# Borders of a two-block transformer's second block in token halves, adds and three pooled tiles on GpSimd, down products waiting row by row

## The chip, the cores and the metric

One core of a Trainium2 chip runs the whole kernel in one launch. The metric is the device time of one execution in microseconds (us). TensorE multiplies matrices into PSUM; VectorE, ScalarE and GpSimd do elementwise work; SyncE issues the loads of weights and the stores of the result. Each engine works through its own queue in order, and they hand work to each other by semaphores.

## The reference

Two transformer blocks in a row, all in float32, width 1024, feed-forward width 2816. The first runs on 512 tokens. The second puts 16 meta tokens in front of them (528 tokens) and has two layers, each the same frame around another mixer:

```python
for i in range(DEPTH_2):                       # i = 0: attention, i = 1: pooling
    a = rmsnorm(h, norm_mix_pre[i])
    m = mla_mixer(a, ...) if i % N_MIXERS == 0 else pool_mixer(a, pool_w_group[j], pool_scale[j])
    h = h + rmsnorm(m, norm_mix_post[i])
    f = conv_ffn(rmsnorm(h, norm_ffn_pre[i]), ffn_w_up[i], ffn_conv_w[i], ffn_conv_b[i], ffn_w_down[i])
    h = h + rmsnorm(f, norm_ffn_post[i])
```

`pool_mixer` takes, for each quarter of the channels, the mean over the last 2, 4, 8 or 16 tokens, subtracts the token itself and multiplies by a 256x256 matrix. `conv_ffn` is an up product, a causal three-tap convolution over tokens, silu(gate) * value, and a down product. `rmsnorm` divides a token by the root of the mean of its squares: a sum over channels, which lie on partitions here.

## The kernel before

Activations lie with channels on partitions and tokens along the free axis, so x is eight tiles of 128 channels by 528 tokens (512 in the first block). An exact float32 product is made of three (`mm3`, L426): both operands are split into a rounded part and its remainder, and w_lo·x_hi, w_hi·x_lo and w_hi·x_hi are added in PSUM. 528 tokens are two spans of 264, so each product of the second block is drawn as two MATMUL rows.

The weights come as a stream of 128x1024 blocks in a ring of four slots (`RING`). For each block SyncE loads `w_raw` (`load_w`), ScalarE rounds it to `w_hi` (`upper`, L883, some 1.04 us) and GpSimd makes the remainder `w_lo` (`lower`, L809, "a lowering" in what follows, some 2.4 us); TensorE waits for `w_lo_ok` of the block and gives the slot back with `w_used`. `STAGES` lists them in order:

```python
    ("dqkv", 6, 1), ("uq", 4, 2), ("uk", 2, 1), ("uv", 2, 1), ("wo", 4, 2),
    ("up_b", 4, 11), ("down_b", 12, 2), ("pool", 2, 1), ("up_c", 4, 11), ("down_c", 12, 2),
```

The numbers are the blocks in one turn of a loop and its turns. A turn fills four PSUM tiles (four output tiles of 128 channels), so `up_b` makes its 44 output tiles in 11 turns and `down_b` its 8 in 2. A block of an up stage or of `wo` holds two rows (2 x 128 input channels) for four output tiles; of the 12 blocks of a down turn ten hold two rows and two hold one (`DOWN_ROWS`: 22 rows in all). Up and down stages of the first block are `up_a` and `down_a`. The four PSUM banks each carry one tile, and `free` counts when one has been read.

Between up and down stands the convolution: per output tile ScalarE takes PSUM with bias (L1099), VectorE adds the three taps (L1563, the longest of its steps) and gates (L1569), ScalarE rounds the result to `mid_hi`, VectorE makes `mid_lo` (L1573). Before the first down product TensorE waits for the whole of it:

```python
                pe.wait_ge(midl_ok, mid0 + KF + 1)
```

After `wo`, `down_b`, `pool` and `down_c` the second block has what is called a border here. ScalarE copies PSUM to `m_out` and squares it (`take_squared`); VectorE adds the squares of the first four tiles (`add_four`, L1595 to L1602); TensorE multiplies ones by that sum and by the last four squares (`norm_four`, L705), which puts the sum over channels in every partition; ScalarE takes Ln and Exp of it and VectorE refines the root into `RS` (`norm`). Then VectorE does all of `post`: for each of eight tiles a product with gain and root (L1611) and the add to x (L1614). A second norm of the new x follows (squares on ScalarE, ones-matmuls at L485), and `split` makes h: product and remainder on VectorE (remainder L1284), rounding on ScalarE. Behind `down_b` the split is that of the pooling (`pooled`, L1699 for its shifted adds), then two blocks of products (`pool`), and a border again before `up_c`. After `down_c` `post` is the last work, and SyncE stores each x tile as it is added.

On GpSimd nothing but lowerings stands from `wo` to the end.

## Time and profile before

| | us |
|---|---|
| median of 3 runs | 2363.22 (2359.76 to 2364.97) |
| span of the profiled execution | 2363.4 |
| TensorE busy in it | 2080.7 |
| VectorE, ScalarE, GpSimd busy | 978.9, 976.8, 836.2 |
| HBM read over it | 183.13 MB, 78 GB/s |

The profile lists one execution. Its span is within 0.2 us of the median of the timed runs. Busy times are those of an engine's own instructions, over the whole span; they say nothing yet of which one is waited for at a given place.

### The profile page before, as it was taken

The page shows a single profiled execution, that of the slowest core. Times are in us where ns is not written, and L with a number is a line of the kernel's source. Part 1 is how long each engine was busy: PE and PEld are TensorE (multiplying, and loading weights), DVE is VectorE, ACT ScalarE, POOL GpSimd, SP SyncE. Part 2 cuts the span into 40 slices and gives each one's busy share as a digit, 9 for nine tenths or more (in the row PEclk, how much of TensorE's full clock was granted, in tenths as well). Part 3 has the DMA queues.
Part 4 walks back from the last instruction along what each step waited for, and adds up shares of the span by engine and source line. Part 5 has one row for each costly group of instructions (what it writes and reads, how often), then busy time and mean ns, then how long its engine had stood idle before and what let it go on. Part 6 is the DMA issues. An engine that isn't in the chain of part 4 may idle for free.

```text
span 2363.4 us, 35671 instructions
## 1 busy us (share of the span) xinstructions
PE 2080.7 (88%) x12776; PEld 1823.4 (77%) x12780; DVE 978.9 (41%) x1644; ACT 976.8 (41%) x1500; POOL 836.2 (35%) x415
## 2 busy tenths in 40 slices
PE   3699999998899989966878897999899659999897
PEld 2587677876577777756767797999899549999896
DVE  5863682114433421155667716242400672424102
ACT  2212673322655542143356634454512344545322
POOL 1244442433244334402643221434334104343341
PEclk7899899999999999988989998999999779999998
DMA  8362001222022222201200011222222102222222
GB/s 295 119 246 101 7 17 38 90 89 71 33 101 89 89 85 101 100 34 45 83 16 0 0 63 36 98 80 98 80 84 101 39 18 89 80 97 80 80 98 80
DMA packets 54263, 185.99 MB, mean 79 GB/s; under 512 B 6848, under 2 KB 8128, under 8 KB 54208
## 3 DMA queue, kind: packets, MB, share of 16 engines
q1 hardware_dynamic: 52768, 183.66, 22.1%
q10 hardware_dynamic: 1440, 1.59, 0.2%
q8 instruction: 35, 0.57, 0.1%
q14 instruction: 20, 0.16, 0.0%
HBM read 183.13 MB, written 2.10 MB: 78 GB/s over the span
## 4 chain that ended last, share of the span: by engine, by line
PE 76%; DVE 13%; issue 5%; ACT 3%; POOL 1%; DMA 1%; DVEq 0%; ACTq 0%; SPq 0%; POOLq 0%
PE PS L426 62%; PE PS L577 3%; PE PS L520 3%; PE PS L646 2%; PE PS L485 1%; PE PS L550 1%; DVE X L1614 1%; DVE small L1413 1%; DVE work L1611 1%; DVE work L1563 1%; PE PS L473 1%; DVE ada_acc L1312 1%; DVE X L1535 1%; PE PS L623 1%; DMA ada_w<-ada 1%
## 5 line engine op out<-in xcount | busy, mean ns | idle before, releaser
L809 POOL TENSOR_TENSOR w_lo<-w_raw,w_hi 128x1024 fp32r<-128x1024 f32 x289 | 697.7, 2418 | 1311.2 <-ACT w_hi L883 1310.0
L883 ACT ACTIVATE w_hi<-w_raw 128x1024 fp32r<-128x1024 f32 x293 | 309.9, 1058 | 884.2 <-PE PS L426 807.7
L426 PE MATMUL PS<-H_hi,w_lo 128*128 128x264 f32 (+1 forms) x2152 | 568.7, 323 | 60.3 <-DVE H_lo L1284 44.9
L426 PE MATMUL PS<-H_hi,w_hi 128*128 128x264 f32 (+1 forms) x2152 | 562.2, 320 | 0.0
L426 PE MATMUL PS<-H_lo,w_hi 128*128 128x264 f32 (+1 forms) x2152 | 561.5, 319 | 0.0
L426 PEld LDWEIGHTS PS<-H_hi,w_lo 128*128 128x128 f32 x2152 | 360.8, 192 | 104.8 <-issue 54.8
L1563 DVE SCALAR_TENSOR_TENSOR work<-PS,vec,work 128x526 f32<-128x526 f32 (+3 forms) x264 | 188.6, 756 | 482.3 <-ACT work L1099 472.5
L426 PEld LDWEIGHTS PS<-H_hi,w_hi 128*128 128x128 f32 x2152 | 360.2, 192 | 27.3
L426 PEld LDWEIGHTS PS<-H_lo,w_hi 128*128 128x128 f32 x2152 | 360.0, 191 | 25.9
L426 PE MATMUL PS<-mid_hi,w_lo 128*128 128x264 f32 (+1 forms) x880 | 215.9, 311 | 21.9 <-DVE mid_lo L1573 20.1
L426 PE MATMUL PS<-mid_hi,w_hi 128*128 128x264 f32 (+1 forms) x880 | 214.5, 309 | 0.0
L426 PE MATMUL PS<-mid_lo,w_hi 128*128 128x264 f32 (+1 forms) x880 | 214.5, 309 | 0.0
L426 PEld LDWEIGHTS PS<-mid_hi,w_lo 128*128 128x128 f32 x880 | 144.7, 191 | 31.3 <-issue 21.0
L426 PEld LDWEIGHTS PS<-mid_lo,w_hi 128*128 128x128 f32 x880 | 144.9, 191 | 7.9
L426 PEld LDWEIGHTS PS<-mid_hi,w_hi 128*128 128x128 f32 x880 | 144.3, 191 | 7.8
L1099 ACT ACTIVATE work<-PS,vec 128x528 f32<-128x528 f32 (+1 forms) x132 | 104.1, 788 | 80.9 <-PE PS L426 80.9
L485 PE MATMUL PS<-work,ones 128*128 128x264 f32 (+1 forms) x212 | 75.7, 512 | 53.2 <-ACT work L929 53.2
L1012 ACT ACTIVATE work<-PS,small 128x128 f32<-128x128 f32 (+5 forms) x144 | 78.6, 546 | 100.9 <-DVE small L1413 100.8
L485 PEld LDWEIGHTS PS<-work,ones 128*128 128x128 f32 x212 | 44.1, 220 | 84.7 <-issue 63.9
L1413 DVE TENSOR_REDUCE small<-PS 128x1 f32<-128x128 f32 (+5 forms) x144 | 73.2, 508 | 49.2 <-PE PS L535 49.1
L520 PE MATMUL PS<-k_hi,q_lo 64*128 64x256 f32 (+2 forms) x192 | 75.4, 393 | 17.2 <-POOL k_lo L835 16.5
L1264 DVE TENSOR_SCALAR work<-PS 128x528 f32<-128x528 f32 (+1 forms) x14 | 9.8, 698 | 194.4 <-ACT work L937 194.4
(212 smaller groups left out, 2924.2 us busy)
## 6 DMA issues: line engine op xcount, KB each, us to landing
w_raw<-stream SPq DMA_DIRECT2D x293, 512.0 KB, 3.2
ada_w<-ada SPq DMA_DIRECT2D x48, 512.0 KB, 5.9
X<-xT SPq DMA_DIRECT2D x1, 2048.0 KB, 8.9
yT<-X SPq DMA_DIRECT2D x8, 256.0 KB, 2.0
rel_raw<-rel ACTq DMA_DIRECT2D x8, 128.0 KB, 2.0
vec<-vecs SPq DMA_DIRECT2D x1, 390.0 KB, 2.8
cos_t<-rope ACTq DMA_DIRECT2D x1, 264.0 KB, 2.5
sin_t<-rope ACTq DMA_DIRECT2D x1, 264.0 KB, 3.0
```

The lines of the kernel that those rows point to most:

```text
L426: last = pe.matmul(out[:, c0 + a:c0 + b], w, x[:, a:b], start=start and i == 0, stop=stop and i == 2)
L473: last = pe.matmul(PS[:, 1, c0 + a:c0 + b], ones[:, :], x[:, a:b], start=k == first, stop=k == n - 1)
L485: last = pe.matmul(PS[:, 0, c0 + a:c0 + b], ones[:, :], square[:, a:b], start=k == 0, stop=k == n - 1)
L520: pe.matmul(out[0:qn, c0 + a:c0 + b], l[rows, o + q0:o + q0 + qn], r[rows, o + a:o + b], start=j == 0, stop=False, skip_group_check=True)
L577: last = pe.matmul(PS[:, 3, 256 + a:256 + b], l[0:kn, vo:vo + P], r[0:kn, so + a:so + b], start=par == 0 and j == 0 and n_ == 0, stop=par ...
L646: last = pe.matmul(PS[:, t, 0:512], l[:, hs], r[:, wr], start=kt == 0 and j == 0, stop=kt == 7 and j == 2)
L809: gp.tensor_tensor(w_lo[:, o], w_raw[:, o], w_hi[:, o].bitcast(F32), ALU.subtract)\
L883: return act_.activation(out, in_, ACT.Copy, scale=scale)
L1012: act_.activation(ht(work, t % 2, S2)[0:qn, 0:ke], PS[0:qn, t % 2, c0:c0 + ke], ACT.Exp, bias=small[0:qn, t % 2:t % 2 + 1], accum_out=smal ...
L1099: act_.activation(ht(work, m, T), psumT(m, T), ACT.Identity, bias=v1("conv", g * 16 + (c + 3)), scale=v1("conv", g * 16 + (c + 2)))\
L1413: v.tensor_reduce(small[0:qn, t % 2:t % 2 + 1], PS[0:qn, t % 2, c0:c0 + ke], AX.X, ALU.max, negate=True).then_inc(nmax_ok, 1)
L1563: ins = v.scalar_tensor_tensor(y[:, s:], u[:, :T - s], w, y[:, s:], ALU.mult, ALU.add)
```

## The change

It touches five things.

- `DOWN_ROWS` puts the two one-row blocks of a down turn first, and the down products wait for `midl_ok` one row at a time, in all three feed-forward parts.
- In the second block the last four weight blocks of `wo`, `down_b` and `down_c` are multiplied twice, each time with half of the tokens (0 to 263, then 264 to 527: half a and half b), and so are the first four blocks behind `wo` and `pool`, and both blocks of `pool` (`tail`, `head`, `pool_half`). The sum of squares of half a stands behind the first block of the second pass.
- Norms, products with gain and root, adds to x, squares and h are made per half, so the operations have 264 columns instead of 528 and there are twice as many.
- The adds to x are GpSimd's (`add_x`, L1077), VectorE keeps the products (`weigh`, L1978).
- GpSimd makes pooled tiles 0, 1 and 2 and their remainders (`pooled_gp`, L1087 to L1112, and `lower_gp`, L1117), VectorE tiles 3 to 7. The result leaves in 16 stores.

The core of the diff; the DVE and ACT parts follow the same order as the GpSimd and PE parts:

```diff
-DOWN_ROWS = (2,) * (KF - 12) + (1,) * (24 - KF)
+DOWN_ROWS = (1,) * (24 - KF) + (2,) * (KF - 12)
...
+HALVES = ((0, HALF2), (HALF2, S2))
...
+POOL_GP = (0, 1, 2)
+POOL_DVE = (3, 4, 5, 6, 7)
...
+            def ffn1(up, down, T, h0):
...
-                pe.wait_ge(midl_ok, mid0 + KF + 1)
...
-                    batch(down, 0, g, g * 12 + BLK0[down], range(12), 4, DOWN_ROWS, 4,
-                          lambda k: (ht(mid_hi, k, T), ht(mid_lo, k, T)), T)
+                    batch(down, 0, g, g * 12 + BLK0[down], range(12), 4, DOWN_ROWS, 4, mid(T), T,
+                          (midl_ok, 1))
...
+                for s in range(2):
+                    done = r0
+                    for b in range(nb - 4, nb):
+                        first, final = b == 0, b == nb - 1
+                        last = half_block(n0 + b, s, rows[b], done, x, first, final,
+                                          begin_tile=(lambda m: begin(name, 0, m, 1)) if first else None,
+                                          told=(4 - s) * final, teller=tail_ok[s])
+                        if s:
+                            last.then_inc(w_used, 1)
+                        done += rows[b]
+                        if s == 1 and b == nb - 4:
+                            sum_squares(name, 0)
...
+            def head(name, before, s, h_base):
+                for b in range(4):
+                    def begin_tile(m):
+                        if s == 0:
+                            bank_free(before, m, 0)
+                        else:
+                            begin(name, 0, m, 0)
+                    def h_wait(k):
+                        pe.wait_ge(hh_ok[s], h_base + k + 1)
+                    last = half_block(BLK0[name] + b, s, 2, 2 * b, hx(S2), b == 0, b == 3,
+                                      begin_tile=begin_tile if b == 0 else None, told=3 * (s == 1 and b == 3),
+                                      teller=full, h_wait=h_wait)
+                    if s == 0 and b == 2:
+                        sum_x_squares(before, 1)
+                    if s:
...
+            def ffn2(up, down, mid0):
+                with pe.Fori(1, 11) as g:
+                    batch(up, 0, g, g * 4 + BLK0[up], range(4), 4, 2, 4, hx(S2), S2)
+                batch(down, 0, 0, BLK0[down], range(12), 4, DOWN_ROWS, 4, mid(S2), S2, (midl_ok, mid0 + 1))
+                tail(down, mid(S2), DOWN_ROWS)
+            batch("wo", 0, 0, BLK0["wo"], range(4), 4, 2, 4, ox2, S2)
+            tail("wo", ox2, (2,) * 4)
+            sum_x_squares("wo", 0)
+            sum_squares("wo", 1)
+            head("up_b", "wo", 0, 0)
+            head("up_b", "wo", 1, 0)
+            ffn2("up_b", "down_b", KF)
+            sum_x_squares("down_b", 0)
+            sum_squares("down_b", 1)
+            pool_half(0)
+            sum_squares("pool", 0)
+            sum_x_squares("down_b", 1)
+            sum_x_squares("pool", 0)
+            pool_half(1)
+            sum_squares("pool", 1)
+            head("up_c", "pool", 0, KD + len(POOL_DVE))
+            head("up_c", "pool", 1, KD + len(POOL_DVE))
+            ffn2("up_c", "down_c", 2 * KF)
...
+            def add_x(name, s):
+                j = TAIL_N[name]
+                for k in range(KD):
+                    gp.wait_ge(wm_ok[s], j * KD + k + 1)
+                    gp.tensor_tensor(hf(X, k, s), hf(X, k, s), hf(work, k % 2, s), ALU.add).then_inc(xh_ok[s], 1)
...
+            def pooled_gp(s):
+                a, b = HALVES[s]
+                gp.wait_ge(rs2_ok[s], 2 * TAIL_N["down_b"] + 2)
+                gp.wait_ge(pad_ok, 2)
+                for k in POOL_GP:
+                    gchain.done(gp.tensor_tensor(padded(k, a, b), X[:, k * S2 + a:k * S2 + b], RS[:, a:b], ALU.mult))
+                for k in POOL_GP:
+                    gchain.wait(2)
+                    gchain.done(gp.tensor_scalar(padded(k, a, b), padded(k, a, b), v1("mix_pre", KD + k),
+                                                 0.5 if k < 2 else 1.0, ALU.mult, ALU.mult))
+                for k in (0, 1):
+                    gchain.wait(2 - k)
+                    a1 = max(a, 1)
+                    gp.tensor_tensor(pool_o[:, k * S2 + a1:k * S2 + b], padded(k, a1 - 1, b - 1), padded(k, a1, b),
+                                     ALU.subtract).then_inc(tp_ok[s], 1)
+                two, four = KD + POOL_SUM0[2], KD + POOL_SUM0[2] + 1
+                gchain.wait()
+                gchain.done(gp.tensor_tensor(padded(two, a, b), padded(2, a, b), padded(2, a - 1, b - 1), ALU.add))
+                gchain.wait()
+                gchain.done(gp.tensor_tensor(padded(four, a, b), padded(two, a, b), padded(two, a - 2, b - 2), ALU.add))
+                gchain.wait()
+                o = pool_o[:, 2 * S2:3 * S2]
+                if s == 0:
+                    i = VEC["cnt"] + 16
+                    gchain.done(gp.tensor_tensor(o[:, 0:16], padded(four, 0, 16), vec[:, i:i + 16], ALU.mult))
+                    a0 = 16
+                else:
+                    a0 = a
+                gchain.done(gp.tensor_scalar(o[:, a0:b], padded(four, a0, b), 0.25, None, ALU.mult))
+                gchain.wait()
+                gp.tensor_tensor(o[:, a:b], o[:, a:b], padded(2, a, b), ALU.subtract).then_inc(tp_ok[s], 1)
...
+            lower_blocks(BLK0["wo"] + RING, BLK0["up_b"])
+            add_x("wo", 0)
+            for b in range(3):
+                lower_one("up_b", b)
+            add_x("wo", 1)
+            lower_blocks(BLK0["up_b"] + 3, BLK0["pool"])
+            add_x("down_b", 0)
+            lower_one("pool", 0)
+            lower_one("pool", 1)
+            pooled_gp(0)
+            lower_one("up_c", 0)
+            lower_gp(0)
+            add_x("down_b", 1)
+            add_x("pool", 0)
+            lower_one("up_c", 1)
+            pooled_gp(1)
+            lower_gp(1)
+            lower_one("up_c", 2)
+            add_x("pool", 1)
+            lower_blocks(BLK0["up_c"] + 3, NBLK)
+            add_x("down_c", 0)
+            add_x("down_c", 1)
...
+            take_first("wo")
+            last_uppers("wo")
+            take_half("wo", 0)
+            root(0, 1)
+            next_upper("wo", 0)
+            square_x("wo", 0, range(0, 4))
+            next_upper("wo", 1)
+            square_x("wo", 0, range(4, 8))
+            next_upper("wo", 2)
+            take_half("wo", 1)
+            next_upper("wo", 3)
+            before_up("wo", 0)
...
-            def post(gain, i0, x0):
...
-                    chain.done(v.scalar_tensor_tensor(w, ht(m_out, k, S2), v1(gain, i0 + k), RS[:, :],
-                                                      ALU.mult, ALU.mult))
-                    chain.wait()
-                    v.tensor_tensor(x2(k), x2(k), w, ALU.add).then_inc(x_ok, 1)
...
+            def weigh(name, s, gain, i0, k):
+                j = TAIL_N[name]
+                if TAILS[name][1] == 8 or k >= 4:
+                    wait_half_out(v, name, s, k if TAILS[name][1] == 8 else k - 4)
+                if k >= 2:
+                    v.wait_ge(xh_ok[s], j * KD + k - 1)
+                v.scalar_tensor_tensor(hf(work, k % 2, s), hf(m_out, k, s), v1(gain, i0 + k), hf(RS, 0, s),
+                                       ALU.mult, ALU.mult).then_inc(wm_ok[s], 1)
...
+            def before_up(name, gain, i0, base, h0, p0):
+                c = 2 * TAIL_N[name]
+                root(0, c + 2)
+                for k in range(KD + 1):
+                    if k < KD:
+                        make_h(0, base, p0, k)
+                    if k == 2:
+                        root(1, c + 1)
+                    if k:
+                        lower_h(0, base, h0, k - 1)
+                    if k >= 3:
+                        weigh(name, 1, gain, i0, k - 3)
+                for k in range(KD - 2, KD):
+                    weigh(name, 1, gain, i0, k)
+                root(1, c + 2)
+                for k in range(KD + 1):
+                    if k < KD:
+                        make_h(1, base, p0, k)
+                    if k:
+                        lower_h(1, base, h0, k - 1)
...
+            def pooled_dve(s):
+                pooled(v, chain, (3,), s, th_ok[s])
+                pooled(v, chain, (4, 5), s, th_ok[s])
+                lower_pooled(s, (3,))
+                pooled(v, chain, (6, 7), s, th_ok[s])
+                lower_pooled(s, (4, 5, 6, 7))
```

What stands in the queues now, at three places. TensorE before the first product of `down_a`, with L680 the wait for the whole of mid (`free0` says that PSUM bank 0 is read), before:

```order
L680 UNCONDITIONAL_BRANCH [waits midl_ok]
L680 ISA
L432 REGISTER_ALU [waits w_lo_ok]
L426 MATMUL PS<-mid_hi,w_lo 128x512 [waits free0]
L426 MATMUL PS<-mid_lo,w_hi 128x512
L426 MATMUL PS<-mid_hi,w_hi 128x512
L426 MATMUL PS<-mid_hi,w_lo 128x512
L426 MATMUL PS<-mid_lo,w_hi 128x512
```

and in the changed kernel:

```order
L772 UNCONDITIONAL_BRANCH
L772 ISA
L522 REGISTER_ALU [waits w_lo_ok]
L516 MATMUL PS<-mid_hi,w_lo 128x512 [waits midl_ok,free0]
L516 MATMUL PS<-mid_lo,w_hi 128x512
L516 MATMUL PS<-mid_hi,w_hi 128x512
L522 REGISTER_ALU
L516 MATMUL PS<-mid_hi,w_lo 128x512 [waits free1]
L516 MATMUL PS<-mid_lo,w_hi 128x512
L516 MATMUL PS<-mid_hi,w_hi 128x512
L516 MATMUL PS<-mid_hi,w_lo 128x512 [waits free2]
```

The wait for `midl_ok` has moved from ahead of the loop to the first product of a row, and with one row in the first block four tiles are begun after three products each.

TensorE at the end of `wo` (OK_hi and OQ_lo are the attention's output, L705 are ones-matmuls), before:

```order
L426 MATMUL PS<-OQ_lo,w_hi 128x264 x2
L426 MATMUL PS<-OK_hi,w_hi 128x264 x2
L770 REGISTER_ALU
L770 COMPARE_AND_BRANCH
L705 MATMUL PS<-RS,ones 128x264 [waits sum4_ok,n_rs,free0]
L705 MATMUL PS<-RS,ones 128x264
L705 MATMUL PS<-work,ones 128x264 [waits n_sq]
L705 MATMUL PS<-work,ones 128x264
```

and in the changed kernel, once in the second pass of the last four blocks and once where the stage ends (`sqx` are squares of x, `mo_a` says that half a of a bank is read, `hh_ok_a` that half a of an h tile is there):

```order
L516 MATMUL PS<-OQ_lo,w_hi 128x264
L516 MATMUL PS<-OK_hi,w_hi 128x264
L806 MATMUL PS<-RS,ones 128x264 [waits sum4_ok,mo_a]
L809 MATMUL PS<-work,ones 128x264 [waits sqm_ok_a] x4
L516 MATMUL PS<-OK_hi,w_lo 128x264 [waits w_lo_ok]
L516 MATMUL PS<-OQ_lo,w_hi 128x264
L516 MATMUL PS<-OK_hi,w_hi 128x264
...
L516 MATMUL PS<-OK_hi,w_hi 128x264
L817 MATMUL PS<-sqx,ones 128x264 [waits sqx_ok_a,mo_a]
L817 MATMUL PS<-sqx,ones 128x264 [waits sqx_ok_a] x7
L806 MATMUL PS<-RS,ones 128x264 [waits sum4_ok,free0]
L809 MATMUL PS<-work,ones 128x264 [waits sqm_ok_b] x4
L516 MATMUL PS<-H_hi,w_lo 128x264 [waits hh_ok_a,mo_a,w_lo_ok]
L516 MATMUL PS<-H_lo,w_hi 128x264
```

The sum of squares of half a has moved in between products of half b; behind the last product stand eight ones-matmuls for the second norm of half a and five for the first norm of half b, and then `up_b` begins with products of half a.

GpSimd behind the attention, before:

```order
L835 TENSOR_TENSOR v_lo<-v_raw,v_hi 128x5x64
L827 REGISTER_ALU
L827 COMPARE_AND_BRANCH
L809 TENSOR_TENSOR w_lo<-w_raw,w_hi 128x1024 [waits w_hi_ok]
L818 UNCONDITIONAL_BRANCH
L818 ISA
L809 TENSOR_TENSOR w_lo<-w_raw,w_hi 128x1024 [waits w_hi_ok]
```

and, in the changed kernel, from `down_b` to the pooling of half b:

```order
L1077 TENSOR_TENSOR X<-X,work 128x264 [waits wm_ok_a] x8
L1009 TENSOR_TENSOR w_lo<-w_raw,w_hi 128x1024 [waits w_hi_ok] x2
L1087 TENSOR_TENSOR pool_s<-X,RS 128x264 [waits pad_ok,rs2_ok_a]
L1087 TENSOR_TENSOR pool_s<-X,RS 128x264 x2
L1090 ISA
L1090 TENSOR_SCALAR pool_s<-pool_s,vec 128x264 [waits gp_step] x3
L1095 TENSOR_TENSOR pool_o<-pool_s 128x263 [waits gp_step] x2
L1099 TENSOR_TENSOR pool_s<-pool_s 128x264 [waits gp_step]
L1101 TENSOR_TENSOR pool_s<-pool_s 128x264 [waits gp_step]
L1106 TENSOR_TENSOR pool_o<-pool_s,vec 128x16 [waits gp_step]
L1110 TENSOR_SCALAR pool_o<-pool_s 128x248
L1112 TENSOR_TENSOR pool_o<-pool_o,pool_s 128x264 [waits gp_step]
L1009 TENSOR_TENSOR w_lo<-w_raw,w_hi 128x1024 [waits w_hi_ok]
L1117 TENSOR_TENSOR H_lo<-pool_o,H_hi 128x264 [waits hi_ok_a] x3
L1077 TENSOR_TENSOR X<-X,work 128x264 [waits wm_ok_b] x8
L1077 TENSOR_TENSOR X<-X,work 128x264 [waits wm_ok_a] x8
L1009 TENSOR_TENSOR w_lo<-w_raw,w_hi 128x1024 [waits w_hi_ok]
L1087 TENSOR_TENSOR pool_s<-X,RS 128x264 [waits pad_ok,rs2_ok_b]
```

Where the loop of lowerings ran on to the end, 24 adds, the 13 steps of half a's pooling and 3 remainders stand among four lowerings, and the pooling's steps wait for one another (`gp_step`).

## Rows read from the trace of the kernel before

**Rows 1.** The page: span, and part 1, busy time of each engine.

```profile
span 2363.4 us, 35671 instructions
PE 2080.7 (88%) x12776; PEld 1823.4 (77%) x12780; DVE 978.9 (41%) x1644; ACT 976.8 (41%) x1500; POOL 836.2 (35%) x415
```

**Rows 2.** Windows over up_b, down_b, gap: busy PE, PEld, DVE, ACT, POOL; PEclk, DMA, GB/s.

```profile
1444.00:1705.00 261.00, 261.00 (x2111) 259.32 (x2110) 93.93 (x136) 134.50 (x153) 102.71 (x43) 0.99 0.25 85
1712.00:1843.00 131.00, 131.00 (x1056) 131.00 (x1057) 4.11 (x3) 31.43 (x35) 56.50 (x24) 0.98 0.26 90
1843.00:1941.00 98.00, 49.89 (x202) 39.27 (x200) 73.54 (x118) 37.72 (x59) 8.18 (x4) 0.75 0.07 25
```

**Rows 3.** Timeline where up_b ends: start, us, engine, line, work [idle before <-releaser].

```profile
1704.40 4.37 DVE L1563 SCALAR_TENSOR_TENSOR work<-PS,vec,work 128x526 f32<-128x526 f32 x6 [0.15 <-DVE work L1563]
1711.81 2.36 POOL L809 TENSOR_TENSOR w_lo<-w_raw,w_hi 128x1024 fp32r<-128x1024 f32 x1 [8.79 <-ACT w_hi L883]
1712.00 0.81 PE L426 MATMUL PS<-mid_hi,w_lo 128*128 128x264 f32 x2 [6.73 <-DVE mid_lo L1573]
```

**Rows 4.** Timeline of the border behind wo, VectorE and GpSimd.

```profile
1394.84 2.59 POOL L809 TENSOR_TENSOR w_lo<-w_raw,w_hi 128x1024 fp32r<-128x1024 f32 x1 [4.56 <-ACT w_hi L883]
1395.21 2.79 DVE L1602 TENSOR_TENSOR RS<-RS,work 128x528 f32<-128x528 f32 x1
...
1424.83 0.71 DVE L1614 TENSOR_TENSOR X<-X,work 128x528 f32<-128x528 f32 x1
1425.45 0.76 DVE L1611 SCALAR_TENSOR_TENSOR work<-m_out,vec,RS 128x528 f32<-128x528 f32 x1
```

**Rows 5.** Groups by form: busy us, mean ns of one | idle before.

```profile
L809 POOL TENSOR_TENSOR w_lo<-w_raw,w_hi 128x1024 fp32r<-128x1024 f32 x289 | 697.7, 2418 | 1311.2 <-ACT w_hi L883 1310.0 <-POOL Q L856 1.2
L883 ACT ACTIVATE w_hi<-w_raw 128x1024 fp32r<-128x1024 f32 x293 | 309.9, 1058 | 884.2 <-PE PS L426 807.7 <-PE PS L646 37.8 <-DMA w_raw<-stream 25.8
...
L835 POOL TENSOR_TENSOR q_lo<-Q,q_hi 128x528 fp32r<-128x528 f32 x16 | 21.1, 1318 | 75.8 <-ACT q_hi L883 75.5 <-ACT k_hi L883 0.3
L835 POOL TENSOR_TENSOR rel_lo<-rel_raw,rel_hi 128x256 fp32r<-128x256 f32 x8 | 5.8, 730 | 5.4 <-ACT rel_hi L883 5.4
...
L1439 DVE TENSOR_TENSOR PT_lo<-PS,PT_hi 128x256 fp32r<-128x256 f32 x32 | 13.2, 412 | 0.0
L883 ACT ACTIVATE PT_hi<-PS 128x288 fp32r<-128x288 f32 x32 | 12.4, 388 | 0.0
```

**Rows 6.** The chain that ended last: the ones-matmuls behind down_b.

```profile
1843.20 4.46 PE PS L705 x20
```

**Rows 7.** Timeline of down_a: TensorE in its middle, VectorE at its end.

```profile
938.04 0.50 PE L426 MATMUL PS<-mid_hi,w_lo 128*128 128x512 f32 x1 [0.70 <-DVE work L1531]
...
940.82 0.50 PE L426 MATMUL PS<-mid_hi,w_lo 128*128 128x512 f32 x1 [1.12 <-DVE work L1531]
...
998.11 2.58 DVE L1535 SCALAR_TENSOR_TENSOR X<-X,work 128x512 f32<-128x512 f32 x1
...
1001.38 2.06 DVE L1535 SCALAR_TENSOR_TENSOR X<-X,work 128x512 f32<-128x512 f32 x1
```

**Rows 8.** Timeline, other stretches: where stages end and begin, and the pooling.

```profile
1415.74 1.05 PE L705 MATMUL PS<-RS,ones 128*128 128x264 f32 x4
...
1443.38 0.56 PE L426 MATMUL PS<-H_hi,w_lo 128*128 128x264 f32 x1 [6.01 <-DVE H_lo L1284]
...
1843.04 0.61 PE L705 MATMUL PS<-RS,ones 128*128 128x264 f32 x2
...
1893.21 1.45 DVE L1699 TENSOR_TENSOR pool_s<-pool_s 128x528 f32<-128x528 f32 x2
...
1941.31 0.56 PE L426 MATMUL PS<-H_hi,w_lo 128*128 128x264 f32 x1 [6.01 <-DVE H_lo L1284]
...
2341.20 0.61 PE L705 MATMUL PS<-RS,ones 128*128 128x264 f32 x2
```

**Rows 9.** Timeline: GpSimd in the first attention's set-up.

```profile
301.39 1.27 POOL L835 TENSOR_TENSOR k_lo<-QK,k_hi 64x512 fp32r<-64x512 f32 x1 [0.24 <-POOL q_lo L835]
```

459 lines of the change are left out of this document (328 added, 131 removed).

## The prediction

> **What bounds the kernel now.** I read the page first [rows 1]: TensorE is busy 88% of 2363.4 us in the profiled execution, so time can only come from where TensorE waits. The windows by stage [rows 2] say where, in the second block: the up and down products run without a hole (261.00 of 261.00 and 131.00 of 131.00 us, granted clock 0.98 to 0.99 of 2.4 GHz). Between `down_b` and `up_c` lie 98 us with 49.89 busy; the rows in order of time add some 28 us between `wo` and `up_b` and 22 behind `down_c` [rows 8], and 7 between each up and its down [rows 3]. The reader is to see that VectorE fills the 98 us (73.54 busy): its chain of norm, add, pooling and norm is what TensorE waits for. Last I read, in order of time too, a norm in which VectorE and GpSimd meet [rows 4]. The profiled span, 2363.4, stands at the median of the runs, 2363.2, so the sum is made from 2363.2.
>
> **Prices for 264 columns.** VectorE with two inputs took 0.412 us for 256 columns [rows 5]: 0.42, and 0.47 where a gain is read too, as 0.76 stands against 0.71 at 528 [rows 4]; an independent one starts 0.09 before the last has ended [rows 4], so 0.35 to 0.40 in a stream. ScalarE 0.388 for 288 [rows 5]: 0.39, 0.33 in a stream. GpSimd 0.730 for 256, 1.318 for 528 [rows 5]: 0.75. TensorE 0.124 per product (131.0/1056 [rows 2]), and 0.446 for one exact ones-matmul (4.46 us for ten of them, each drawn as two rows) [rows 6].
>
> **GpSimd and VectorE exclude each other.** A two-input add on VectorE beside a lowering took 2.79 us instead of 0.71, and ended 0.57 behind GpSimd's end; the lowering itself, asked for while VectorE was in such an add, took 2.59 [rows 4] where their mean is 2.42 [rows 5]. So all that the change puts on GpSimd adds to VectorE's two-input time: a product and an add cost 0.35 + 0.75, 1.1 us a tile and half, 8.9 for eight, where the kernel before takes 0.76 and 0.71 less the overlap, some 1.4 for a whole tile [rows 4], 0.7 a half. The Trainium skill, SBUF — State Buffer, "Who interferes with whom", says the same as a rule: the pair of ports is an exclusive lock, and the second to issue fully blocks. By that rule the trace agrees.
>
> **1. Down waits row by row, three junctions.** TensorE stood 6.73 us until `mid_lo` of the last group [rows 3]. Now it waits for a bank only. VectorE's taps run from 1704.40, 0.68 apart: bank 0 is free at 1705.2, bank 1 at 1705.9, bank 2 at about 1708.0, bank 3 at 1708.8. A tile of a one-row block is six products, 0.74 us, so tiles 0 and 1 fill to 1706.8 and tile 2 waits 1.2. Some 1.4 us stay: 5.3 saved, three times 15.9. The last rows land at 1712.0, and are wanted 60 us later. The ring of four holds 1+1+2+2 rows, 17.8 us, against ScalarE's queue, which is clear at 1711.8, when GpSimd gets its block [rows 3]. Bounds: 12 (4.0 each) and 18.
>
> **2. The end of `down_a`.** Its last two blocks had one row, 2.8 us, and lowerings came back to back into VectorE's residual: 2.58 and 2.06 for 512 columns, 0.69 by the 0.71 of 528 [rows 4, 7], and TensorE stood 0.70 and 1.12 us in the middle [rows 7]. With two rows last, a block takes 5.7 us and a lowering meets one or two residuals, not the queue of them: 1.8 in the middle, and 2.7 of the 3.3 at the end. 4.5; bounds 0 and 5.
>
> **3. `wo` to `up_b`.** Call 0 the first ones-matmul of before, 1415.74 [rows 8]. The last four blocks are now two passes of 96 x 0.124 = 11.9 us with a sum of five ones-matmuls, 2.2, inside the second. So the last product ends at +2.2 and half a is complete at 2.2 - 11.9 - 2.2 = -11.9. Its sum stands behind one block of the second pass (24 products, 3.0): -8.9 to -6.7. Root: Ln and Exp 0.42 each, three VectorE operations 0.46 each, hops: -4.1. Eight products and adds at 1.1: +4.8. What is queued behind these adds on GpSimd are three lowerings of `up_b`, and SyncE's loads behind those. ScalarE has, behind the squares of half a, two weight roundings (1.06 by their mean [rows 5], 0.96 in a stream) and eight reads of half b (0.33 each), 4.6 us, before it may start the second root, which takes 2.7 more with its wait for the sum: +12.9. Product, rounding and remainder of the first tile, 0.47 + 0.42 + 0.42 and hops, 2.0: the first product of `up_b` at +14.9. Before it came at +27.6 [rows 8]. That is 12.7 us earlier. But the 2112 products of up, 261 us before, now hold 3.6 us of b's sum of x² (8 x 0.446); half a's 72 first products wait 2.9 on tiles of h that cost VectorE 0.35 for the product, 0.35 for the remainder, 0.35 for half b's product and 0.75 of GpSimd's add; then 1.5 until half b's h, and 1.3 for a lowering that stood behind GpSimd's adds: 9.3. Net 3.4 saved. Bounds: 0 (nothing of the lead survives) and 7 (the holes of 5.7 go, and some).
>
> **4. `down_b` to `up_c`.** 0 is now 1843.04 [rows 8], and the start is the same: adds of half a from -4.1 to +4.9, second root at +12.4 (before, both norms were done at about +25). Then, in order of VectorE's queue:
> - Pooling of half a. VectorE has 26 full-width sums and products, 10 of 16 columns and 5 remainders; GpSimd 12 short ones of 264, one of 16, one lowering (2.4) and 3 remainders. GpSimd's run in turn with VectorE's: 15 x (0.75 + 0.22 of waiting) + 2.4 = 17; the rest of VectorE's behind it, 15 x 0.38 + 10 x 0.15 = 7.2; with hops 24.5: +37.
> - Root of half b 1.7, its eight products and adds 8.9, and 1.6 until the last squares: +49.
> - Root of the pool's half a, 2, and its eight adds, 8.9: +60.
> - Root of x in half b. A lowering of `up_c` takes the lock in the middle of it, 2.4: +63.
> - Pooling of half b, the same without the 16-column steps, 21: +84.
> - The pool's products of half b, 8 squares and 8 reads of ScalarE (0.33 to 0.4 each), a lowering, eight ones-matmuls and a root: +94. The first tile of h: first `up_c` product at +95.5.
>
> Before it came at 1941.31, +98.3 [rows 8]. So 2.8 us earlier, and again 9.3 lost inside the two passes of up, less an estimated 0.3 for a granted clock of 0.75 over the gap before [rows 2], which would be up sooner: 6.2 us slower. This is where the work on GpSimd is paid for: VectorE's 73.54 us become about 64, but some 60 of GpSimd can't lie beside them. Bounds: 10 faster (GpSimd hidden for half its time) and 20 slower (0.25 more for each of some 50 operations, and a hop each).
>
> **5. The end.** 22.2 us from the last sum of squares to the end [rows 1, 8]. Now half b: 2.2 later by the inserted sum, four weight roundings of ScalarE (0.96 each) ahead of the root, but eight adds at 1.1 instead of sixteen operations at 0.71, and a root at half width: 0.4 saved; bounds -3 and 3. The 16 output transfers of half the size replace 8; the first eight go out under half b, and the last is issued by its add as before.
>
> **Sum.** 15.9 + 4.5 + 3.4 - 6.2 + 0.4 = 18.0 us: 2363.2 - 18.0 = 2345. Unseen costs: GpSimd's one-input TENSOR_SCALAR, eight of them, taken at a two-input's 0.75 (nearest rows, and both bounds are its 256 columns 0.73 and a full 528 1.32: -0.2 to +4.6 us in all); reads at a shifted column, taken at nothing, as two shifted adds of VectorE took 1.45, 0.73 each [rows 8]. The Trainium skill, GPSIMD Engine Reference, "Engine selection", puts one-input operations at roughly line rate; by that the eight would be near 0.4 us as an estimate and the sum 2.6 better. No run here shows it.
>
> **Rivals.**
> - *The lock doesn't bite on short operations.* Then eight adds take 8 x 0.75 = 6, hidden under VectorE, and pooling overlaps: 1.1 to 0.75 over 64 adds is some 15 on the path, the two poolings 5 each: 25 us more, 2320. For it: no row has both engines in short ones. Against: the rows of 528 [rows 4] leave no overlap. Chance 0.10.
> - *The junctions give nothing.* A one-row block first leaves less cover, and the down product waits for a lowering that comes at 1711.81 + 2.36 [rows 3] and then each 2.4: against 17.8 us of blocks from 1705.3 there are 9 to spare, so I give it little. 2361. Chance 0.07.
> - *Slower: short GpSimd operations are dearer in a chain.* About 75 of 95 stand on the path. The hop after GpSimd was 0.24 where it waited for itself [rows 9]. At 0.25 us more each, 0.99 instead of 0.75, 18.8 us go and it decides; at 0.35 more the time is 2371. For it: per column the short form already costs more than the long (730/256 against 2418/1024 [rows 5]). Chance 0.08.
> - *Something in between*, half a junction lost or half a lock, 2352 to 2360: 0.07, of which 0.02 within 0.2%.
>
> **How the numbers follow.** The forecast, all five terms near their values, 2336 to 2354, has 0.68. The range 2328 to 2359 adds the milder parts of the neighbours and leaves out half of the first and most of the second and third rival, 0.2. What a measurement here can tell from no change is 0.2%, 4.7 us. Faster: 0.68 + 0.10 + 0.05 of the cases between + 0.02 of the second rival, where a part of the junctions stays = 0.85. Same: the other 0.05 of that rival and 0.02 between = 0.07. Slower 0.08.
>
> **What would show it.** At the junctions TensorE idles under 2 us for a bank. In the windows, `down_b` to `up_c` stays within a few us of 98 while VectorE's two-input operations read 0.9 to 1.1 us instead of 0.42, and GpSimd's adds 0.75 to 0.9. The first up product comes 12 us sooner after `wo`, and up takes 9 longer. VectorE rows of 0.42 beside GpSimd rows would prove the first rival; adds at 1 us with VectorE idle the slow one. I would be wrong above all by GpSimd's length, 7.5 us for each 0.1, and by the order in which the two take the lock.

## The result, and the profile after

The changed kernel took 2323.95 us (median of 4 runs, 2320.99 to 2328.26) beside 2362.18 for the kernel before: a ratio of 0.9842 with a 95% interval of 0.9827 to 0.9856, 38 us faster. The forecast was 18 us faster, 2345, in a range of 2328 to 2359: the direction was right, the size half of what was measured, and the time lies below the range. The profiled execution of the changed kernel took 2328.26 and has a span of 2326.4, so its trace shows 37.0 of the 38 us [rows 1].

The page of the changed kernel, span and part 1, against [rows 1]:

```profile
span 2326.4 us, 35857 instructions
PE 2070.3 (89%) x12792; PEld 1814.9 (78%) x12792; DVE 992.0 (43%) x1711; ACT 989.1 (43%) x1602; POOL 915.1 (39%) x510
```

GpSimd is busy 79 us longer and VectorE 13 us longer, and yet the kernel is faster. The windows of the changed kernel over the rest of `up_b`, `down_b` without its last pass, and from `down_b` to `up_c`, with the columns of [rows 2]:

```profile
1436.00:1688.00 252.00, 250.41 (x2034) 248.38 (x2032) 93.38 (x141) 133.57 (x155) 102.70 (x43) 1.00 0.29 90
1688.00:1809.00 121.00, 119.81 (x981) 119.53 (x981) 10.22 (x12) 35.54 (x44) 50.76 (x21) 1.00 0.30 95
1821.00:1905.00 84.00, 42.35 (x186) 35.15 (x184) 60.16 (x114) 37.91 (x94) 51.64 (x54) 0.78 0.09 32
```

The third row answers to the 98 us of [rows 2]: VectorE's 73.54 busy us have become 60.16, GpSimd's 8.18 have become 51.64, and the stretch is 13 us shorter. The second row shows a granted clock of 1.00 where `down_b` had 0.98.

TensorE and VectorE of the changed kernel at the end of `up_b`, in order of time, against [rows 3]:

```profile
1688.10 0.48 PE L516 MATMUL PS<-mid_hi,w_lo 128*128 128x264 f32 x2
...
1690.99 0.51 PE L516 MATMUL PS<-mid_hi,w_lo 128*128 128x264 f32 x2 [1.19 <-DVE work L1918]
...
1693.15 1.46 DVE L1928 TENSOR_TENSOR mid_lo<-work,mid_hi 128x528 f32 x2 [0.32 <-ACT mid_hi L1155]
```

The wait of 6.73 us is gone, 1.19 for a PSUM bank is left, and the last rows of mid come while down runs. And VectorE and GpSimd in the row of products and adds behind `wo`:

```profile
1401.24 1.37 DVE L1978 SCALAR_TENSOR_TENSOR work<-m_out,vec,RS 128x264 f32<-128x264 f32 x2 [0.64 <-POOL X L1077]
1403.33 1.30 DVE L1978 SCALAR_TENSOR_TENSOR work<-m_out,vec,RS 128x264 f32<-128x264 f32 x2 [0.72 <-POOL X L1077]
1405.36 1.31 DVE L1978 SCALAR_TENSOR_TENSOR work<-m_out,vec,RS 128x264 f32<-128x264 f32 x2 [0.72 <-POOL X L1077]
...
1402.29 1.65 POOL L1077 TENSOR_TENSOR X<-X,work 128x264 f32<-128x264 f32 x2 [0.37 <-DVE work L1978]
1404.31 1.65 POOL L1077 TENSOR_TENSOR X<-X,work 128x264 f32<-128x264 f32 x2 [0.37 <-DVE work L1978]
1406.34 1.63 POOL L1077 TENSOR_TENSOR X<-X,work 128x264 f32<-128x264 f32 x2 [0.37 <-DVE work L1978]
1407.93 6.97 POOL L1009 TENSOR_TENSOR w_lo<-w_raw,w_hi 128x1024 fp32r<-128x1024 f32 x3
```

GpSimd's pairs of adds repeat every 2.02 to 2.03 us, 1.01 a tile, and each engine waits for the other in turn. The three lowerings of `up_b` stand behind the eighth add.

From the rows at which stages end and begin, in the two profiled executions (us from the last product of one stage, taken where the ones-matmuls behind it start, to the first of the next, the 2.2 us of the sum of squares that was inserted into a stage counted with the border behind it; `down_b` to `up_c` before: 1843.04 to 1941.31 [rows 8], after: 1820.64 to 1905.38 and 2.2):

| part | forecast saved | before | after | saved |
|---|---|---|---|---|
| `up_a`'s end over `down_a` to `dqkv` | 5.3 + 4.5 | 176.8 | 166.4 | 10.4 |
| `up_b`'s end to `down_b`'s, and the same in c | 5.3 each | 137.8 each | 130.3 each | 7.5 each |
| `wo` | 0 | 49.7 | 48.3 | 1.4 |
| `wo` to `up_b` | 12.7 | 27.6 | 14.0 | 13.6 |
| `up_b` itself | -9.3 | 261.9 | 270.4 | -8.5 |
| `down_b` to `up_c` | 2.8 | 98.3 | 86.9 | 11.3 |
| `up_c` itself | -9.3 + 0.3 | 262.1 | 270.5 | -8.4 |
| `down_c` to the end | 0.4 | 22.2 | 20.2 | 2.0 |

The forecast column adds up to 18.0, the last to 36.8. An up stage "itself" is from its first product to its last.

### The profile page after: what moved, and what is told of

Same layout as the page of the kernel before. It is cut to its first block, busy times and chain, and to the rows that moved or that the text cites. A ratio compares the mean times of both kernels' runs of the same rounds, so it can differ in the third digit from the quotient of the medians.

```text
span 2326.4 us, 35857 instructions
## 1 busy us (share of the span) xinstructions
PE 2070.3 (89%) x12792; PEld 1814.9 (78%) x12792; DVE 992.0 (43%) x1711; ACT 989.1 (43%) x1602; POOL 915.1 (39%) x510
## 3 DMA queue, kind: packets, MB, share of 16 engines
q1 hardware_dynamic: 53920, 183.66, 24.5%
## 4 chain that ended last, share of the span: by engine, by line
PE 76%; DVE 12%; issue 5%; ACT 4%; POOL 2%; DMA 1%; DVEq 0%; ACTq 0%; POOLq 0%; SPq 0%
PE PS L516 62%; PE PS L667 3%; PE PS L610 3%; PE PS L736 2%; PE PS L640 1%; PE PS L575 1%; DVE work L1918 1%; DVE small L1768 1%; PE PS L563 1%; DVE ada_acc L1667 1%; DVE pool_s L292 1%; DMA ada_w<-ada 1%; POOL X L1077 1%; PE PS L960 1%; DVE work L1978 1%
## 5 line engine op out<-in xcount | busy, mean ns | idle before, releaser
L516 PE MATMUL PS<-H_hi,w_lo 128*128 128x264 f32 (+1 forms) x2152 | 583.3, 323 | 67.9 <-POOL H_lo L1117 27.5
L516 PE MATMUL PS<-H_hi,w_hi 128*128 128x264 f32 (+1 forms) x2152 | 576.0, 320 | 0.0
L516 PE MATMUL PS<-H_lo,w_hi 128*128 128x264 f32 (+1 forms) x2152 | 575.1, 319 | 0.0
L516 PEld LDWEIGHTS PS<-H_lo,w_hi 128*128 128x128 f32 x2152 | 366.5, 192 | 25.8
L516 PE MATMUL PS<-mid_hi,w_lo 128*128 128x264 f32 (+1 forms) x880 | 223.8, 308 | 3.6 <-DVE work L1918 3.6
L516 PE MATMUL PS<-mid_hi,w_hi 128*128 128x264 f32 (+1 forms) x880 | 222.8, 306 | 0.0
L516 PE MATMUL PS<-mid_lo,w_hi 128*128 128x264 f32 (+1 forms) x880 | 222.3, 306 | 0.0
L1768 DVE TENSOR_REDUCE small<-PS 128x1 f32<-128x128 f32 (+5 forms) x144 | 73.2, 509 | 49.4 <-PE PS L625 49.3
L1077 POOL TENSOR_TENSOR X<-X,work 128x264 f32<-128x264 f32 x64 | 53.8, 856 | 97.0 <-DVE work L1978 97.0
L640 PE MATMUL PS<-ident,work 128*128 128x128 f32 (+2 forms) x400 | 69.1, 280 | 23.6 <-DVE work L1779 22.4
L575 PE MATMUL PS<-work,ones 128*128 128x512 f32 (+1 forms) x116 | 47.0, 563 | 32.1 <-ACT work L1201 32.1
```

What stands on the lines that cost most here:

```text
L516: last = pe.matmul(out[:, c0 + a:c0 + b], w, x[:, a:b], start=start and i == 0, stop=stop and i == 2)
L575: last = pe.matmul(PS[:, 0, c0 + a:c0 + b], ones[:, :], square[:, a:b], start=k == 0, stop=k == n - 1)
L640: last = pe.transpose(PS[0:kn, 2, o:o + qn], pb[0:qn, k0:k0 + kn], ident[0:qn, 0:qn])
L1077: gp.tensor_tensor(hf(X, k, s), hf(X, k, s), hf(work, k % 2, s), ALU.add).then_inc(xh_ok[s], 1)
L1768: v.tensor_reduce(small[0:qn, t % 2:t % 2 + 1], PS[0:qn, t % 2, c0:c0 + ke], AX.X, ALU.max, negate=True).then_inc(nmax_ok, 1)
```

## The experiments

Ratios are to the kernel before, timed beside each.

**b_junction.** The kernel before with the first part of the change alone.

```diff
-DOWN_ROWS = (2,) * (KF - 12) + (1,) * (24 - KF)
+DOWN_ROWS = (1,) * (24 - KF) + (2,) * (KF - 12)
...
-                                pe.wait_ge(h_ok, h_ready + kt + 1)
+                                pe.wait_ge(r_sem or h_ok, h_ready + kt + 1)
...
-                pe.wait_ge(midl_ok, mid0 + KF + 1)
...
-                          lambda k: (ht(mid_hi, k, T), ht(mid_lo, k, T)), T)
+                          lambda k: (ht(mid_hi, k, T), ht(mid_lo, k, T)), T, mid0 + 1, midl_ok)
```

> The kernel before with the change's first part alone: down products wait for midl_ok row by row, one-row blocks first. Theory 1 (the prediction's terms 1 and 2): TensorE's wait of 6.7 us at each junction shrinks to 1.4, and the end of down_a gains 4.5: 15.9 + 4.5, about 20 us faster than before, 2342. Theory 2 (the wait also cost granted clock: the first 5 us of down products ran at 0.50): each junction gives 5.5 of wait and 2 of clock, with 3.8 at down_a some 26 us faster, 2336. The rest of the whole change (38 us) would then be worth 12 and not 18.

Measured: 2337.0 us, 0.9888 (0.9872 to 0.9903), 25 us faster. That is two thirds of the whole gain, and theory 2. The same stretch as above, `up_b`'s end to `down_b`'s, is 7.6 us shorter, of which the wait explains 5.5. The windows over `down_b` say where the rest is. Before, over the wait and the first 10 us behind it:

```profile
1705.00:1712.00 7.00, 0.27 (x4) 0.06 (x2) 6.21 (x10) 5.77 (x8) 0.19 (x1) 0.87 0.11 42
1712.00:1717.00 5.00, 5.00 (x22) 5.00 (x23) 0.00 (x0) 1.04 (x1) 2.17 (x1) 0.50 0.29 103
1717.00:1722.00 5.00, 5.00 (x42) 5.00 (x42) 0.00 (x0) 1.06 (x1) 0.42 (x1) 1.00 0.01 5
```

and with the junction alone, over the whole of `down_b`:

```profile
1693.50:1823.50 130.00, 128.79 (x1055) 128.58 (x1056) 10.02 (x12) 39.63 (x45) 57.96 (x24) 1.00 0.29 97
```

After 6.73 idle us TensorE's granted clock stood at 0.50, its level of 1.2 GHz, for the next 5 us: 22 product rows where the following 5 us hold 42. That is 20 rows of 0.12, over 2 us lost on top of the wait. The kernel before shows the same behind its waits for `mid` in the first block and in `up_c`:

```profile
872.40:877.40 5.00, 4.98 (x12) 3.93 (x13) 0.00 (x0) 1.09 (x1) 2.23 (x1) 0.51 0.27 105
2210.10:2215.10 5.00, 4.96 (x22) 4.97 (x23) 0.00 (x0) 1.07 (x1) 2.21 (x1) 0.50 0.31 103
```

After the 1.21 idle us of b_junction it stayed at 1.00. The mean of 0.98 over 131 us [rows 2] had hidden it.

**b_waits_only.** The same with `DOWN_ROWS` left as it was (two-row blocks first).

> As b_junction, but the one-row blocks stay last. The first block of a turn has then two rows, a tile takes 1.5 us instead of 0.74, and tile 2 comes after its bank is free: no wait at all is left at the junctions. Theory 1: 3 x 6.7, 20 us faster than before, nothing at the end of down_a. Theory 2: 3 x (6.7 + 2.1), 26 us, as much as b_junction, so that the order of the rows gives nothing in sum. If the order helps the end of down_a as the prediction had it (4.5) and costs 1.2 at each junction, the two kernels lie within 1 us of each other.

Measured: 2335.57 us, 0.9890 (0.9875 to 0.9905), 26 us faster, the same as b_junction. In the traces `down_b` is 1.5 us shorter (128.93 against 130.41 from first product to last, no wait for a bank), `down_c` as much, and the stretch behind `down_a` is 2.1 us longer and `down_a` 0.7. The order of the rows pays at one place, `down_a`, what it costs at the other two. The row by row wait is the whole of the gain.

**b_warm.** The kernel before keeps its wait, and TensorE works in it (on ones, the results overwritten).

```diff
+                pe.wait_ge(free[0], FREE0[down][0] + 1)
+                for i in range(24):
+                    pe.matmul(PS[:, 0, 0:128], ones[:, :], ones[:, 0:128], start=True, stop=True)
                 pe.wait_ge(midl_ok, mid0 + KF + 1)
```

> The kernel before with its wait for the whole of mid kept, but TensorE multiplies ones by ones (24 products of 128 columns into the free bank 0, results overwritten) while it waits. Theory 1: the wait is all that the junction costs, so the time stays at 2362. Theory 2: the granted clock stays at 1.0 behind the wait, the first 18 products of down take 0.12 us instead of 0.22, and each junction gives 2 us: 6 us faster, 2356.

Measured: 2357.07 us, 0.9980 (0.9971 to 0.9989), 5.0 us faster by work that is thrown away. Windows over the wait and the first 5 us of down products in b_warm:

```profile
1702.00:1708.70 6.70, 5.58 (x49) 5.39 (x48) 5.95 (x9) 5.74 (x8) 0.15 (x1) 1.00 0.06 24
1708.70:1713.70 5.00, 4.96 (x40) 4.97 (x41) 0.00 (x0) 1.07 (x1) 2.23 (x1) 1.00 0.29 93
```

The stretch from the last up product to the first down product is 6.73 us as before, and `down_b` takes 129.01 instead of 131.21, `down_c` 128.99 instead of 131.22, `down_a` 124.70 instead of 126.94: 2.2 each, 6.7 in sum; the interval of the timed runs, some 2.6 to 6.9 us, holds that sum. So the granted clock is a cost of its own.

**b_bench.** A bench behind the last add of the kernel before; the weights' buffers are its inputs. Per phase, VectorE and GpSimd run so many operations, with a barrier between phases. A phase lists for VectorE and then for GpSimd the kind, the columns and the number of operations; "tt" adds two tensors in SBUF, "ts" is a TENSOR_SCALAR with one tensor input, "ps" an add with one input in PSUM.

```diff
+        PHASES = (("tt", 264, 16, None, 0, 0), (None, 0, 0, "tt", 264, 8), ("tt", 264, 16, "tt", 264, 8),
+                  ("tt", 528, 8, "tt", 528, 4), ("tt", 264, 16, "tt", 1024, 3), (None, 0, 0, "ts", 264, 8),
+                  ("tt", 264, 16, "ts", 264, 8), ("ts", 264, 16, None, 0, 0), ("ts", 264, 16, "tt", 264, 8),
+                  ("ps", 264, 16, "tt", 264, 8), ("tt", 528, 8, None, 0, 0), (None, 0, 0, "tt", 528, 4))
```

> The kernel before with a bench behind its last add: VectorE and GpSimd in independent operations, alone and together, phase by phase with a barrier between. Widths 264, 528 and 1024. Theory A (the prediction's): each excludes the other for a whole operation: 16 VectorE adds (0.35 each) and 8 GpSimd adds (0.75 each) of 264 together take 16 x 0.35 + 8 x 0.75 = 11.6 us. Theory B (the rival): no exclusion on short operations, they take the longer of the two, 6 us. Theory C: exclusion only while data streams, some 0.27 of VectorE's 0.35 and some 0.5 of GpSimd's 0.75: 16 x 0.27 + 8 x 0.5, about 8.5 us. With GpSimd's input a lowering of 1024 columns, VectorE's short adds stand still for its whole 2.4 us in A and C alike. GpSimd's one-input operation: 0.75 by the prediction; VectorE from PSUM beside GpSimd: as alone.

It ran once, 2443.8 us with the bench; what counts are its rows, in order of time for VectorE (phases 1, 8 and 9 in one row, 10 and 11) and then for GpSimd (phases 2 to 7, 9, 10 and 12):

```profile
2358.55 5.59 DVE L303 TENSOR_TENSOR m_out<-w_hi 128x264 f32<-128x264 f32 x16 [0.23 <-DVEq L1746]
...
2412.94 12.62 DVE L299 TENSOR_SCALAR m_out<-w_hi,vec 128x264 f32<-128x264 f32 x32 [0.38 <-POOL XC L299]
2425.60 5.52 DVE L301 TENSOR_TENSOR m_out<-PS,w_hi 128x264 f32<-128x264 f32 x16
2431.38 5.04 DVE L303 TENSOR_TENSOR m_out<-w_hi 128x528 f32<-128x528 f32 x8 [0.26 <-POOL XC L303]
...
2364.36 5.61 POOL L303 TENSOR_TENSOR XC<-w_lo 128x264 f32<-128x264 f32 x8 [39.55 <-DVE m_out L303]
2370.43 6.95 POOL L303 TENSOR_TENSOR XC<-w_lo 128x264 f32<-128x264 f32 x8 [0.46 <-POOL XC L303]
2380.16 6.97 POOL L303 TENSOR_TENSOR XC<-w_lo 128x528 f32<-128x528 f32 x4 [2.77 <-DVE m_out L303]
2389.63 7.56 POOL L303 TENSOR_TENSOR XC<-w_lo 128x1024 f32<-128x1024 f32 x3 [2.50 <-DVE m_out L303]
2401.70 3.70 POOL L299 TENSOR_SCALAR XC<-w_lo,vec 128x264 f32<-128x264 f32 x8 [4.51 <-DVE m_out L303]
2405.57 7.26 POOL L299 TENSOR_SCALAR XC<-w_lo,vec 128x264 f32<-128x264 f32 x8 [0.17 <-POOL XC L299]
2417.54 6.01 POOL L303 TENSOR_TENSOR XC<-w_lo 128x264 f32<-128x264 f32 x8 [4.70 <-DVE m_out L299]
2425.65 5.63 POOL L303 TENSOR_TENSOR XC<-w_lo 128x264 f32<-128x264 f32 x8 [2.10 <-DVE m_out L299]
2436.65 5.05 POOL L303 TENSOR_TENSOR XC<-w_lo 128x528 f32<-128x528 f32 x4 [5.37 <-DVE m_out L303]
```

Alone, an add of 264 columns costs VectorE 0.35 and GpSimd 0.70. Together GpSimd's eight take 6.95 (0.87 each by their mean), and GpSimd starts its next phase, behind VectorE's sixteenth, 9.7 us after the first: between theory A's 11.6 and C's 8.5, and far from B's 6. In 6.95 us VectorE made nine, the other seven took the 2.77 us for which GpSimd then waited: they go in turn, and a pair costs 0.87 where the durations add up to 1.05. At 528 columns a pair costs 1.74 where 0.63 and 1.26 add up to 1.89. So the exclusion holds for short operations, less 0.15 to 0.18 per pair. The Trainium skill, SBUF — State Buffer, "Who interferes with whom", has the lock as exclusive; the bench agrees, but for that overlap. With one of VectorE's inputs in PSUM both run as alone (5.52 and 5.63). One-input operations of GpSimd cost 0.46 alone and 0.91 beside VectorE's adds. A one-input operation on VectorE isn't free of GpSimd either: VectorE's TENSOR_SCALAR costs 0.27 alone (sixteen from 2412.94 until GpSimd starts its phase 9), and GpSimd's eight adds beside them took 6.01, 0.75 for a pair. The Trainium skill, GPSIMD Engine Reference, "Engine selection", puts GpSimd's one-input operations at roughly line rate and its two-input ones about twice as slow as VectorE's. The bench agrees on the second, 0.70 against 0.35 alone; with one tensor input it was 0.46 against VectorE's 0.27.

**a_add_dve.** The changed kernel with the add to x back on VectorE, behind its product.

```diff
                 for k in range(KD):
-                    gp.wait_ge(wm_ok[s], j * KD + k + 1)
-                    gp.tensor_tensor(hf(X, k, s), hf(X, k, s), hf(work, k % 2, s), ALU.add).then_inc(xh_ok[s], 1)
...
                                        ALU.mult, ALU.mult).then_inc(wm_ok[s], 1)
+                v.wait_ge(wm_ok[s], j * KD + k + 1)
+                v.tensor_tensor(hf(X, k, s), hf(X, k, s), hf(work, k % 2, s), ALU.add).then_inc(xh_ok[s], 1)
```

> The changed kernel with the adds to x back on VectorE: product, wait for it, add, tile by tile and still in halves. Theory S (GpSimd's adds stop VectorE for most of their length, so moving them gives nothing): a tile and half costs 0.93 us (two dependent VectorE operations at 0.46) where product and GpSimd's add now repeat every 1.01; over five rows of eight on the path 3 us faster than the changed kernel, and up to 1 lost where h tiles stand between: 2321 to 2325. Theory M (taking the adds off VectorE is a real gain): each add returns 0.35 to 0.42 us to VectorE's chain, 40 of them on the path, 14 to 17 us slower, about 2339.

Measured: 2330.89 us, 0.9863 (0.9848 to 0.9878), slower than the changed kernel by some 5 to 7 us in median, with intervals that overlap. The stages are clearer (table below): 3.0 lost behind `wo`, 4.1 behind `down_b`, 1.1 won at the end. Neither theory holds: S had the sign wrong, and M's 14 to 17 us were 7 or less and came, as the rows show, from something else. The row of eight behind `wo` on VectorE, and GpSimd beside it:

```profile
1397.05 2.50 DVE L1976 SCALAR_TENSOR_TENSOR work<-m_out,vec,RS 128x264 f32<-128x264 f32 x1
...
1399.94 0.49 DVE L1976 SCALAR_TENSOR_TENSOR work<-m_out,vec,RS 128x264 f32<-128x264 f32 x1
1400.46 0.43 DVE L1979 TENSOR_TENSOR X<-X,work 128x264 f32<-128x264 f32 x1
1400.81 0.49 DVE L1976 SCALAR_TENSOR_TENSOR work<-m_out,vec,RS 128x264 f32<-128x264 f32 x1
...
1404.30 2.58 DVE L1976 SCALAR_TENSOR_TENSOR work<-m_out,vec,RS 128x264 f32<-128x264 f32 x1
...
1396.64 2.63 POOL L1009 TENSOR_TENSOR w_lo<-w_raw,w_hi 128x1024 fp32r<-128x1024 f32 x1 [13.87 <-ACT w_hi L1153]
1404.13 2.47 POOL L1009 TENSOR_TENSOR w_lo<-w_raw,w_hi 128x1024 fp32r<-128x1024 f32 x1 [4.86 <-ACT w_hi L1153]
```

Undisturbed, a tile takes 0.87 us on VectorE alone, less than the 1.01 with GpSimd. But GpSimd, free of adds, goes on with its lowerings as soon as their weights are rounded, and each holds up a product by 2 us.

**a_pool_dve.** The changed kernel with all pooled tiles on VectorE.

```diff
-POOL_GP = (0, 1, 2)
-POOL_DVE = (3, 4, 5, 6, 7)
+POOL_GP = ()
+POOL_DVE = (0, 1, 2, 3, 4, 5, 6, 7)
...
-            pooled_gp(0)
...
-            pooled_gp(1)
```

> The changed kernel with all eight pooled tiles and their remainders on VectorE, GpSimd only lowers. Theory S: the pooling of a half is then 44 VectorE operations at 0.35 and, in half a, 16 short ones at 0.1, 17.5 and 15.5 us, where it took 21 and 17.5 with both engines: some 5 us faster than the changed kernel, 2319; as little as 2 if lowerings now fall into it. Theory M: the 13 and 12 steps and 3 remainders that GpSimd made were hidden in part; VectorE's share grows by 16 operations of 0.35 a half, 2 x 5.6, so 8 to 11 us slower, 2333.

Measured: 2321.5 us, 0.9826 (0.9812 to 0.984), not told apart from the changed kernel by its time, but its `down_b` to `up_c` is 3.05 us shorter. From the root to the last remainder half a took 17.9 us (21.0 with both engines) and half b 15.7 (17.5). Half b, in whose pooling neither kernel has a lowering, shows the tiles alone: 1.8. In half a something else moved too. The changed kernel has a lowering of `up_c` in the middle of VectorE's pooling:

```profile
1840.59 2.53 POOL L1009 TENSOR_TENSOR w_lo<-w_raw,w_hi 128x1024 fp32r<-128x1024 f32 x1
1840.84 2.57 DVE L285 SCALAR_TENSOR_TENSOR pool_s<-X,vec,RS 128x264 f32<-128x264 f32 x1
```

Here it comes ahead of the pooling and holds up a step of the root instead (1.77 for 0.43):

```profile
1819.05 6.97 POOL L1009 TENSOR_TENSOR w_lo<-w_raw,w_hi 128x1024 fp32r<-128x1024 f32 x3
1824.54 1.77 DVE L1962 SCALAR_TENSOR_TENSOR work<-work 128x264 f32<-128x264 f32 x1
```

By the stages, the three tiles given to GpSimd cost more than they relieve; how much of half a's 3.1 us is the tiles and how much the lowering's place was not separated.

**a_none_gp.** Both edits together.

> Both: halves and row by row waits, but neither adds nor pooled tiles on GpSimd. Theory S: the two gains add, 4 to 9 us faster than the changed kernel, 2315 to 2320, and the halves alone are then worth the whole of the 12 us that the junctions leave and more. Theory M: 20 us or more slower than the changed kernel, 2345, which is slower than the kernel before with the junctions alone (2337).

Measured: 2326.51 us, 0.9851 (0.9837 to 0.9864). The two don't add: behind `wo` it loses what a_add_dve lost (table below). But it says what the token halves are worth by themselves, with the row by row waits and everything but lowerings off GpSimd: against b_junction (2337.0, 0.9872 to 0.9903) it is some 10 us faster, with intervals that lie apart.

**a_warm.** The changed kernel with products of ones in three waits: eight behind the last sum of squares after `wo`, ten ahead of each half of `pool`.

```diff
+            def keep_busy(n, s):
+                for _ in range(n):
+                    pe.matmul(psum_half(3, s), ones[:, :], vec[:, 0:HALF2], start=True, stop=True)
```

> The changed kernel with products of ones in three of TensorE's waits (8 behind wo's last sum of squares, 10 ahead of each half of pool, into a bank that is free, results overwritten). Where the clock is 0.50 at a start, the products of half a pool stage (96 rows) take 0.22 instead of 0.12. Theory clock: both pool halves end 3 to 4 us sooner, of which ScalarE's and VectorE's queues leave about half, and up_b begins 1 us sooner in its second block: 3 to 7 us faster, 2317 to 2321. Theory wait (the pool stage and the heads wait for VectorE's tiles, whatever the clock): no change within 2 us of 2324, or slower if the extra products hold up the real ones.

Measured: 2326.72 us, 0.9857 (0.9842 to 0.9872), no gain. The waits of its TensorE over the two pool halves:

```profile
PE PS L516 <- ACT m_out L1168: 8.3, 2, 4.2
PE PS L873 <- ACT H_hi L1168: 5.7, 1, 5.7
PE PS L817 <- ACT sqx L1283: 3.6, 4, 1.4
```

(us in total, times, longest.) The first block of a pool half ran at 1.00, then TensorE waited 4 us for ScalarE to read its banks and the second block ran at 0.62 in the mean. There the clock follows the waits, and the waits set the time; `down_b` to `up_c` was 1.0 us longer.

**a_add_gated.** As a_add_dve, and GpSimd waits where it added.

```diff
-                for k in range(KD):
-                    gp.wait_ge(wm_ok[s], j * KD + k + 1)
-                    gp.tensor_tensor(hf(X, k, s), hf(X, k, s), hf(work, k % 2, s), ALU.add).then_inc(xh_ok[s], 1)
+                gp.wait_ge(xh_ok[s], (j + 1) * KD)
```

> As a_add_dve (adds to x back on VectorE), but GpSimd, where it added before, now waits until VectorE has added all eight tiles of the half, and only then goes on with its lowerings. Theory Q (the adds on GpSimd helped by what they kept out: lowerings, each of which held a VectorE product for 2.5 us in a_add_dve): with the lowerings kept out and a tile at 0.87 us on VectorE against 1.01 before, up_b starts 10.7 us after wo's last product (11.8 in the changed kernel, 14.8 in a_add_dve) and up_c 81 to 82 after down_b's (84.7 and 88.9); 4 to 6 us faster than the changed kernel, 2319. Theory M (an engine of its own for the adds is the gain): as a_add_dve, 2331.

Measured: 2323.16 us, 0.9834 (0.982 to 0.9847). Against a_add_dve (0.9863, 0.9848 to 0.9878) an idle GpSimd makes the kernel faster, by intervals that are just apart. `up_b` starts 10.73 us after `wo`'s last product, as expected; `up_c` starts at 83.2 and not at 81 to 82.

**a_gated.** As a_add_gated, with all pooled tiles on VectorE.

> As a_add_gated, and all pooled tiles on VectorE: GpSimd does nothing but lowerings, at the places that the changed kernel gave them. Theory Q: the gain of a_add_gated and the 3 us of a_pool_dve together, up_c starts 78 to 79 us after down_b's last product, 7 to 9 us faster than the changed kernel, 2316. If the two gains don't add (a lowering or ScalarE's reads take the place), 81 and 2320.

Measured: 2319.71 us (2318.68 to 2322.23), 0.9820 (0.9807 to 0.9833), the lowest of all, though not told apart from a_pool_dve (0.9826). It is apart from a_none_gp (0.9851, 0.9837 to 0.9864), from which it differs by GpSimd's wait alone. Against the changed kernel the intervals overlap a little; by stages it is 1.1, 3.2 and 1.1 us shorter. The gains added in part only: 81.55.

From the traces, us (last product to first product, and to the end):

| kernel | `wo` to `up_b` | `down_b` to `up_c` | `down_c` to the end |
|---|---|---|---|
| changed | 11.82 | 84.74 | 17.9 |
| a_add_dve | 14.80 | 88.87 | 16.8 |
| a_pool_dve | 11.81 | 81.69 | 17.9 |
| a_none_gp | 14.79 | 83.25 | 16.8 |
| a_add_gated | 10.73 | 83.19 | 16.8 |
| a_gated | 10.74 | 81.55 | 16.8 |

A stage ends where the ones-matmuls behind its last product start, 1820.64 in the changed kernel and 1816.18 in a_gated for `down_b`; the first products of `up_c` are, in this order:

```profile
1905.38 0.36 PE L516 MATMUL PS<-H_hi,w_lo 128*128 128x264 f32 x1 [2.01 <-DVE H_lo L1989]
```

```profile
1897.73 0.36 PE L516 MATMUL PS<-H_hi,w_lo 128*128 128x264 f32 x1 [2.00 <-DVE H_lo L1987]
```

## Why the prediction was wrong

**Where it failed.** The steps were the right ones, and each went the way forecast but one, term 4. Two things were priced wrong, both in the same direction: the junctions' half-speed products were put at nothing, and a GpSimd operation beside a VectorE one was put too dear.

1. *Terms 1 and 2, the junctions and `down_a`: 20.4 forecast, 25.4 in the trace, 25 by b_junction alone.* The remaining wait was put at 1.4 and is 1.2. What was missing is the granted clock. The step "some 1.4 us stay: 5.3 saved" counted idle time only; the half-speed rows behind it cost 2.2 more, three times (b_warm). That is 6.7, more than the 5.0 by which the two terms were exceeded. The price stood in the trace and was averaged away in the 0.98 of one long window. Term 2 in itself was too high: of the 10.4 us around `down_a`, 7.6 are wait and clock as at the other two junctions, and 2.8 are left for its 4.5.

2. *Term 4, `down_b` to `up_c` and the passes of `up_c`: 6.2 slower forecast, 2.9 faster measured.* The failing step is "all that the change puts on GpSimd adds to VectorE's two-input time". A pair was priced at the sum of two durations, 1.1; it costs 0.87 in the bench's stream and 1.01 in the kernel's chain, where each also waits for the other. Over three rows of eight that is 2. In the two poolings, priced at 24.5 and 21, it is 3.5 each: 21.0 and 17.5 were measured. In half a GpSimd's steps ended 16.1 us after the pooling's start and not 17, and VectorE had 4.9 left behind them and not 7.2. The assumed 0.75 for a one-input operation (0.46 alone, 0.71 here) is a part of that; the shares were not taken apart. The 9.3 us lost in the two passes of `up_b` and `up_c` came out right, 8.5 and 8.4.

3. *Term 3, `wo` to `up_b`: 3.4 forecast, 5.1 measured.* The first product came at +14.0 and not at +14.9, with the row of adds at 1.01 a tile, and the loss inside `up_b` was 8.5 and not 9.3. Another 1.4 lie in `wo` itself, for which nothing was forecast: its first 10 us had a granted clock of 0.85 in the one profile and 0.69 in the other, behind a wait of 1.4 and 1.7 us. It isn't chance, as `wo` takes 48.2 to 48.3 in the seven traces with halves and 49.4 to 49.7 in the five without, but why it differs was not tried.

4. *Term 5: 0.4 forecast, 2.0 measured.* The row of eight at 1.01 and not 1.1 is 0.7 of it; the other 0.9 was not taken apart.

**The rivals.** "The lock doesn't bite on short operations", with 2320 the nearest in time, was wrong as a mechanism: in b_bench no two-input pair of 264 or 528 columns overlaps by more than 0.18 us. That the time came near it is luck: the clock, which no rival named, gave nearly 7 us, and term 4 was 9.1 too slow for reasons that leave the lock in place. "The junctions give nothing" is refuted by b_junction. "Short GpSimd operations are dearer in a chain" is refuted as far as 0.25 each goes: the 64 adds read 0.86 each by their mean on the page and not 0.75, and GpSimd waits 0.37 for VectorE ahead of each pair, but those waits lie beside VectorE's work and the pair comes to 1.01.

**What was right, but only half seen.** "This is where the work on GpSimd is paid for" holds: with that work taken back and its queue held, the kernel is as fast or faster (a_gated, 2319.7), so none of the 38 us needs the adds and tiles on GpSimd: the row by row waits give 25, and with the token halves it is 35 (a_none_gp) or, with GpSimd's queue held as well, 44 (a_gated). What I had called a cost of the adds, "three lowerings of `up_b`" queued behind them, is the one use of them that the stages show. An engine in order that is kept from its lowerings doesn't collide with VectorE; a_add_dve and a_add_gated differ by that alone, 4.1 and 5.7 us in the two borders.

## What to carry to other kernels

Price an idle stretch of TensorE by the rows behind it too: look at the granted clock in narrow windows right after each wait, not in the mean of a stage. Before moving work from VectorE to GpSimd, add the pair's durations (the bench's pair came out 0.15 to 0.18 us below that sum) and don't take the larger of the two, unless one of VectorE's inputs lies in PSUM; and look which long GpSimd operations can start beside a short VectorE chain, since the place in GpSimd's queue can be worth more than who adds.

## What the runs showed of the hardware

- After 6.6 to 6.7 idle us TensorE's granted clock was 0.50 to 0.51 over its next 5 busy us in three places; after 1.2 idle us it stayed at 1.00 (b_junction). Products of ones in the same 6.7 us kept it at 1.00 and brought 2.2 us at each place.
- Two-input operations of VectorE and GpSimd in SBUF alternate: 0.87 us for a pair of 264 columns (0.35 and 0.70 alone), 1.74 for a pair of 528 (0.63 and 1.26 alone). With one of VectorE's inputs in PSUM they took 0.35 and 0.70 side by side.
- GpSimd's TENSOR_SCALAR with one tensor input took 0.46 us for 264 columns where its two-input add took 0.70, and 0.91 when VectorE added beside it. VectorE's TENSOR_SCALAR took 0.27 alone, and a pair of it and GpSimd's add 0.75.
